# Embedding projection weights moved to a buffer of their own, with first loads, first rounding and last stores reordered

## The reference

```python
def first_block(x, p, ...):
    for i in range(DEPTH):                       # DEPTH = 2
        m = hybrid_mixer(x, ...) if i % 2 == 0 else mla_mixer(x, ...)
        h = layer_norm(DN_ALPHA * x + m, ln1_g[i], ln1_b[i])
        f = jnp.square(jax.nn.relu(h @ mlp_w1[i])) @ mlp_w2[i]
        e = jax.nn.sigmoid(h @ ple_w_gate[i]) * (p[i] @ ple_w_proj[i])   # p[i]: 512 x 256
        x = layer_norm(DN_ALPHA * h + f + e, ln2_g[i], ln2_b[i])
    return x

def second_block(x, c, ctx, ...):
    for layer in range(DEPTH):
        mod_l = (silu(c) @ ada_w[layer] + ada_b[layer]).reshape(batch, 1, 6, D_MODEL)
        ...                                      # mixer with mLSTM, window and full attention
        x = x + mod_l[:, :, 5] * sq_relu_mlp(modulate(x, norm2_g[layer], mod_l, 3), mlp_w1[layer], mlp_w2[layer])
    return x
```

## Time and profile before

| | |
|---|---|
| Runs | 3247.15, 3251.91, 3253.18 us; median 3251.91 us |
| Profiled execution | 3252.88 us, of which the span from the first to the last instruction is 3251.1 us |
| Mean granted TensorE clock | 0.969 of full |
| PE busy | 3072.2 us (94%) |
| DVE, ACT, POOL busy | 1634.8 us (50%), 1233.7 us (38%), 154.0 us (5%) |
| Chain that ended last | PE 86%, DVE 6%, ACT 3%, issue 1%, DMA 1% of the span |

### The profile page before, as it was taken

One profiled execution on the slowest core, in us unless ns is written; L12 is line 12 of the kernel. 1 busy time (PEld: TensorE's weight loads), 2 busy tenths in 40 slices (PEclk: granted clock), 3 DMA queues, 4 the chain that ended last, 5 costly groups with the idle time before them and its releaser, 6 DMA issues.

```text
span 3251.1 us, 39508 instructions
## 1 busy us (share of the span) xinstructions
PE 3072.2 (94%) x15144; PEld 2480.5 (76%) x15144; DVE 1634.8 (50%) x2438; ACT 1233.7 (38%) x2046; POOL 154.0 (5%) x142
## 2 busy tenths in 40 slices
PE   6989999999998999998998998999999899899999
PEld 5676687876776788776885777788888776778887
DVE  4864576775454567775316543433333534344344
ACT  2453233335563233336114442422222344443332
POOL 2300000011000000010002002000000100000000
PEclk9969999999999999999998999999999999999999
DMA  5101434433201344431211001112111110022221
GB/s 193 53 1 58 170 135 180 170 117 52 78 1 58 142 162 181 155 110 40 65 41 38 1 1 52 53 52 77 52 56 73 52 52 27 1 84 97 103 95 59
DMA packets 157680, 259.19 MB, mean 80 GB/s; under 512 B 54333, under 2 KB 70075, under 8 KB 157437
## 3 DMA queue, kind: packets, MB, share of 16 engines
q1 hardware_dynamic: 155812, 252.66, 22.3%
q10 hardware_dynamic: 1628, 4.78, 0.4%
q0 software_dynamic: 128, 0.26, 0.0%
HBM read 255.59 MB, written 2.10 MB: 79 GB/s over the span
## 4 chain that ended last, share of the span: by engine, by line
PE 86%; DVE 6%; ACT 3%; issue 1%; DVEq 1%; DMA 1%; ACTq 1%; POOLq 0%; PEldq 0%; PEld 0%; SPq 0%
PE psA L779 23%; PE psA L780 22%; PE psA L781 22%; PE psB L744 3%; PE psA L730 3%; PE psA L905 3%; PE psO L922 2%; ACT work L1282 2%; PE psO L867 1%; PE psA L966 1%; ACT w_hi L1282 1%; PE psA L795 1%; DVE work L2078 1%; DMA wbuf<-in_hy_w_in_dram 1%; PE psA L797 1%
## 5 line engine op out<-in xcount | busy, mean ns | idle before, releaser
L1282 ACT ACTIVATE w_hi<-wbuf 128x1024 fp32r<-128x1024 f32 (+1 forms) x349 | 368.1, 1057 | 1205.5 <-PE psA L781 1141.6
L779 PE MATMUL psA<-act_hi,w_hi 128*128 128x512 f32 (+1 forms) x1872 | 709.9, 379 | 61.0 <-DVE act_lo L1975 37.6
L1969 DVE TENSOR_TENSOR w_lo<-wbuf,w_hi 128x1024 fp32r<-128x1024 f32 (+1 forms) x349 | 430.3, 1236 | 556.9 <-ACT w_hi L1282 551.9
L780 PE MATMUL psA<-act_lo,w_hi 128*128 128x512 f32 (+1 forms) x1872 | 702.3, 375 | 0.0
L781 PE MATMUL psA<-act_hi,w_lo 128*128 128x512 f32 (+1 forms) x1872 | 700.7, 374 | 0.0
L779 PE MATMUL psA<-hid_hi,w_hi 128*128 128x512 f32 (+1 forms) x1280 | 477.1, 373 | 5.4 <-DVE work L2078 4.5
L780 PE MATMUL psA<-hid_lo,w_hi 128*128 128x512 f32 (+1 forms) x1280 | 472.2, 369 | 0.0
L781 PE MATMUL psA<-hid_hi,w_lo 128*128 128x512 f32 (+1 forms) x1280 | 471.4, 368 | 0.0
L779 PEld LDWEIGHTS psA<-act_hi,w_hi 128*128 128x128 f32 x1872 | 358.9, 192 | 134.3 <-issue 53.3
L780 PEld LDWEIGHTS psA<-act_lo,w_hi 128*128 128x128 f32 x1872 | 358.9, 192 | 62.1 <-issue 1.7
L781 PEld LDWEIGHTS psA<-act_hi,w_lo 128*128 128x128 f32 x1872 | 358.1, 191 | 63.0
(11 more groups left out here) (280 smaller groups left out, 3520.7 us busy)
## 6 DMA issues: line engine op xcount, KB each, us to landing
wbuf<-in_mlp_w_dram SPq DMA_DIRECT2D x64, 2048.0 KB, 8.4
work<-in_ada_w_dram SPq DMA_DIRECT2D x32, 1536.0 KB, 11.2
wbuf<-in_ab_w_in_dram SPq DMA_DIRECT2D x10, 1024.0 KB, 5.1
wbuf<-in_ple_w_gate_dram SPq DMA_DIRECT2D x4, 2048.0 KB, 7.8
wbuf<-in_hy_w_in_dram SPq DMA_DIRECT2D x3, 2048.0 KB, 14.3
wbuf<-in_c_w_in_dram SPq DMA_DIRECT2D x3, 2048.0 KB, 7.8
wbuf<-in_hy_w_out_dram SPq DMA_DIRECT2D x2, 2048.0 KB, 7.8
wbuf<-in_mla_w_out_dram SPq DMA_DIRECT2D x2, 2048.0 KB, 8.1
```

The lines of the kernel that those rows point to most:

```text
L779: pe.matmul(psA[:, s, a:b], w_hi, x_hi[:, a:b], start=first, stop=False)
L780: pe.matmul(psA[:, s, a:b], w_hi, x_lo[:, a:b], start=False, stop=False)
L1282: return nc.scalar.activation(out, in_, func, **kw)
L1969: tt(split_target(wL, stage, u), unit(v, stage, u, g), split_target(wH, stage, u), ALU.subtract).then_inc(S["w_split"], 1)
```

## The change

Three parts. (1) `ple_w_proj` is no longer in the ring: it has 8 KB per partition of working memory of its own (`ple_w`), loaded in one piece ahead of the gate's first chunk once the mixer's output has been split. The products `ple_p` 0 to 3 move into the layer norm: number 0 ahead of the sum of squares, 1 to 3 behind it, into four banks of `psB` and `psO`; DVE multiplies and adds these four between the splits of the gate's weights. Products 4 to 7 stay behind the gate. DVE splits the first two units of the MLP ahead of them, not behind them. (2) At the start a first piece of 256 columns of weights is loaded behind `x` by itself; `ctx`, `p` and the constants are issued only when ACT has split all of `x`; `x` is split tile by tile between the copies, the two first weight units after tiles 2 and 3, and the barrier is gone. (3) The last group of `mlp3` is written out behind the loop, and the transposes of the output stand between its products; ACT copies them to `rows_out` by feature tile, and SP stores four blocks of 256 columns (1 KB per row) in place of four blocks of 128 rows of 4 KB.

The diff, cut to what matters:

```diff
-        chunk("hy", ("split", "hy_xb", 1), (0, *tile_cols(w, 0, 512)))
+        first_w = (wbuf[:, 0, :, 0:256], tile_cols(w, 0, 256)[0])
+        chunk("hy", ("split", "hy_xb", 1), (256, *tile_cols(w, 256, 512)))
...
             for c in range(2):
                 chunk(f"ple{l}", ("split", f"ple_g{l}", 4 * c + 3), (0, *tile_cols(d["ple_w_gate"][l], c * 512, c * 512 + 512)))
-            for c in range(2):
-                chunk(f"ple{l}", (f"ple_p{l}", 4 * c + 3),
-                      (0, *tile_cols(d["ple_w_proj"][l], c * 512, c * 512 + 512, 2)))
...
+        PLE_EARLY = 4
+        ple_banks = [psB[:, 0, :], psB[:, 1, :], psO[:, 512:1024], psO[:, 0:512]]
...
             sp.dma_start(xn, d["x"][0].rearrange("(a p) d -> p a d", p=P)).then_inc(x_in, 16)
+            sp.dma_start(*first_w).then_inc(first_w_in, 16)
...
+                if n in (first_chunk["ple0"], first_chunk["ple1"]):
+                    l = 0 if n == first_chunk["ple0"] else 1
+                    sp.wait_ge(S["act_split"], BASE_X[("hy_out", "mla_out")[l]] + KD)
+                    sp.dma_start(ple_w, d["ple_w_proj"][l].rearrange("(k p) c -> p k c", p=P)).then_inc(ple_w_in, 16)
...
             for t in range(LT):
-                sp.wait_ge(out_set, t + 1)
-                sp.dma_start(out[0][t * P:t * P + P], xn[:, t, :]).then_inc(out_stored, 16)
+                sp.wait_ge(out_set, 2 * t + 2)
+                part = slice(2 * t * P, 2 * t * P + 2 * P)
+                sp.dma_start(out[0].rearrange("(a p) d -> p a d", p=P)[:, :, part], rows_out[:, :, part]).then_inc(out_stored, 16)
...
+            def ple_early(l, js):
+
+                pe.wait_ge(ple_w_in, 16 * (l + 1))
+                for j in js:
+                    if j < 2:
+                        turned(pe, ("dsa_o", "mla_o")[l], (2, 6)[l] + j)
+                    if j == 3:
+                        pe.wait_ge(S["mean_read"], 2 * l + 1)
+                    for k in range(2):
+                        ins = pe.matmul(ple_banks[j], ple_w[:, k, j * P:j * P + P], pT[:, l, k, :],
+                                        start=(k == 0), stop=(k == 1))
+                    ins.then_inc(S["ple_early"], 1)
+
+            def norm_beside_ple(i):
+
+                ple_early(i // 2, [0])
+                layer_norm(i)
+                ple_early(i // 2, range(1, PLE_EARLY))
...
+                def turn_out(j):
+
+                    pe.wait_ge(S["residual_set"], KD + j + 1)
+                    turn("out", j, [(t * P, xT[:, j, t * P:t * P + P]) for t in range(LT)])
...
                         split_products(name, [j0], n, operands, more, [range(GH)])
+                        if leaves:
+                            turn_out(2 * q - 2)
...
+                        if leaves:
+                            turn_out(2 * q - 1)
...
+                leaves = name == "mlp3"
+                with pe.Fori(1 if paired else 0, GROUPS - 1 if leaves else GROUPS) as i:
                     group(i, False)
+                if leaves:
+                    group(GROUPS - 1, False, True)
+                    turn_out(KD - 2)
+                    turn_out(KD - 1)
...
                 split_linear(f"ple_g{l}", sH[LAT], sL[LAT], LAT, split_here(f"mlp{l}"))
-                linear(f"ple_p{l}", f"ple{l}", 2, pT[:, l], LAT, kt=2)
+                for j in range(PLE_EARLY, KD):
+                    product(f"ple_p{l}", j - PLE_EARLY, features(ple_w, j * P, pT[:, l], LAT, 2))
...
             for k in range(KD):
                 turn("load", k, [(t * P, xn[:, t, k * P:k * P + P]) for t in range(LT)])
-            meet(pe)
...
-            layer_norm(0, xT)
+            norm_beside_ple(0)
...
+            def split_first():
+
+                for k in range(KD):
+                    turned(act, "load", k)
+                    f(xH[:, k, :], xT[:, k, 0:LAT], ACT.Copy).then_inc(S["act_hi"], 1)
+                    if k in (2, 3):
+                        w_hi("hy_xa", k - 2)
+
             act.dma_start(const[:, 0:P], consts[:, 0:P]).then_inc(ident_in, 16)
+            split_first()
             act.dma_start(cn, d["ctx_2"][0].rearrange("(a p) d -> p a d", p=P)).then_inc(c_in, 16)
             for l in range(2):
                 act.dma_start(pn[:, l], d["p"][l, 0].rearrange("(a p) d -> p a d", p=P)).then_inc(p_in, 16)
             act.dma_start(const[:, P:], consts[:, P:NCONST]).then_inc(const_in, 16)
-            w_hi("hy_xa", 0)
-            w_hi("hy_xa", 1)
-            meet(act)
...
+            for j in range(KD):
+                ps, free = get_b(act, "out", j)
+                f(rows_out[:, :, j * P:j * P + P], ps.rearrange("p (t c) -> p t c", c=P), ACT.Copy).then_inc(free, 1)
+                act.drain().then_inc(out_set, 1)
...
             def ple(l):
-                split_linear(f"ple_g{l}", start=2)
-                for j in range(KD):
+                def gated_early(j):
+                    if j >= PLE_EARLY:
+                        return
                     emptied(v, f"ple_g{l}", j)
-                    ps, free = get_a(v, f"ple_p{l}", j)
+                    v.wait_ge(S["ple_early"], PLE_EARLY * l + j + 1)
+                    tt(gates[:, j, :], gates[:, j, :], ple_banks[j], ALU.mult)
+                    v.drain()
+                    stt(acc[:, j, :], acc[:, j, :], ALPHA, gates[:, j, :], ALU.mult, ALU.add)
+
+                split_linear(f"ple_g{l}", gated_early, start=2)
+                w_lo(f"mlp{l}", 0)
+                w_lo(f"mlp{l}", 1)
+                for j in range(PLE_EARLY, KD):
+                    emptied(v, f"ple_g{l}", j)
+                    ps, free = get_a(v, f"ple_p{l}", j - PLE_EARLY)
                     tt(gates[:, j, :], gates[:, j, :], ps[:, 0:LAT], ALU.mult).then_inc(free, 1)
                     v.drain()
                     stt(acc[:, j, :], acc[:, j, :], ALPHA, gates[:, j, :], ALU.mult, ALU.add)
                 v.drain().then_inc(S["ple_set"], 1)
-                w_lo(f"mlp{l}", 0)
-                w_lo(f"mlp{l}", 1)
...
             for k in range(KD):
                 ps, free = get_b(v, "load", k)
                 nc.vector.tensor_copy(xT[:, k, 0:LAT], ps).then_inc(free, 1)
-            w_lo("hy_xa", 0)
-            w_lo("hy_xa", 1)
-            meet(v)
+                if k >= 1:
+                    x_lo("hy", k - 1, xT, xH, xL)
+                if k in (2, 3):
+                    w_lo("hy_xa", k - 2)
+            x_lo("hy", KD - 1, xT, xH, xL)
...
             mlp("mlp3", 3, LAT)
-            for t in range(LT):
-                for e in range(2):
-                    ps, free = get_b(v, "out", 2 * t + e)
-                    nc.vector.tensor_copy(xn[:, t, 512 * e:512 * e + 512], ps).then_inc(free, 1)
-                v.drain().then_inc(out_set, 1)
```

42 lines of the change are left out of this document (17 added, 25 removed).

## The result

The changed kernel takes 3222.85 us (median of 4 runs, 3221.17 to 3223.06) against 3249.53 us of the kernel before on the same chip (3247.15 to 3253.18): a ratio of 0.9916, with a 95% interval of 0.9904 to 0.9928. The forecast was 3221. The profiled execution took 3223.06 us, with a span of 3221.2. One run of the last experiment took 4445 us at a mean granted clock of 0.64, in a slow state that says nothing of the code, and is left out of its median.

The account below looks back on a forecast made before the run. PE, busy 94% of the span, bounds the kernel, so only its standing or half-clock time can be won. 19.6 + 4.5 + 3.2 + 1.6 + 2.6 = 31.5 us gives 3221 against 3251.9; own range 3216 to 3227.

Parts of the forecast that it names:

- Handover: Gate to MLP, both layers: PE starts the MLP at T + 8.3 instead of T + 18.1; 9.8 us a layer, 19.6 in all.
- First MLP unit at full clock: First MLP unit, both layers: PE never stands over 1.4 us, so units of 8.03 and 7.35 take 5.45; 4.5 us.
- Norm: First norm, both layers: products fill PE's wait and the clock stays up; 1.6 us a layer, 3.2 in all, from 0.
- Start: Kernel start: `x` lands at 9.2, first product at 23.2 instead of 24.76; 1.6 us won, from -0.6 to 5.
- My sentence that the clock was at its full level before the first transpose: Kernel start: the trace could not test the skill page's rule on transposes, since the clock was already full; no size given.
- rival B: Start gives more: clock up when PE starts the pair saves 2.7 us, sooner `x` up to 5 in all; 3216, chance 0.13.
- End: After the last product: most output transposes move between products, 9.4 us against 12.0; 2.6 us won, between -0.3 and 3.3.
- The 0.4 us for shorter rows: Final store: 0.4 us more, since a 512 KB store now has rows of a quarter the length.
- D: Long stages: denser PE work makes the chip grant less clock; at two points 3282 us; chance 0.03.
- A: Norm and handover: the stall goes but half clock stays, so 4.5 + 3.2 us are not won; 3229, chance 0.14.
- C: Handover: the MLP's first weights still come late because SP is held, so 24.1 us are missing; 3245, chance 0.04.

Follow-up runs that it names:

- the last experiment: Changed kernel, but in layer 1 the MLP's first weights issue only at the gate's end and DVE's low parts follow its pairs: 3226.27 us (median of 3).
- experiment 4: Changed kernel, but all eight projection products stand behind the gate and the MLP's first low parts behind DVE's last pair: 3245.44 us (11 runs).
- experiment 5: Changed kernel, but all eight projection products stand behind the gate, with both MLP low parts ahead of DVE's eight pairs: 3235.26 us (one run).
- the end alone: Kernel before with only the new end (transposes between last products, copies on ACT, stores by columns): 3245.02 us (11 runs), ratio 0.9988.
- the start alone: Kernel before with only the new start (loads, splitting, barriers): 3245.6 us (median of 11 runs), ratio 0.9997.
- both orders: Changed kernel with the MLP's second low part behind the four pairs and the first weights' splits placed later at the start: 3215.11 us (4 runs).
- experiment 8: Changed kernel with two extra matmuls in layer 1 (3223.27 us), with four (3231.97), unchanged again (3222.13), and with layer 1's MLP weights issued late (3226.27).
- the second trace of the changed kernel: Changed kernel run once more, nothing altered: median 3222.13 us; the profiled execution took 3227.75 us.

## Why the prediction was right

**Handover: right, 19.6 us.** The MLP starts at T + 8.3 as worked out, T being the gate's end, and the one wait left is that of product 6 for DVE. What the working did not say is how the 9.8 us part: by experiments 4 and 5 the transfer taken away alone gives little, and the four products moved into the norm, once it is gone, give most.

**First MLP unit at full clock: 4.5 forecast.** True in the changed kernel (5.5 us in both layers), but the code of before loses less there than its one trace said: in layer 0 the first unit took 8.03 us in that trace and 7.15 in the trace of the end alone. Against the trace of the end alone both handovers with their first units give 11.2 + 11.5 = 22.7 us, beside 24.1 for the two terms together.

**Norm: the term that failed.** The step said that the clock stays up and each norm gains 1.6. The clock stays up. But the second trace with the old norm is itself 1.3 us faster there, because its clock is back before the last tile is split; then both kernels wait for that tile, and in layer 0 nothing is gained. In layer 1 it is 0.8 us (lead from 18.7 to 19.5). So the two norms gave some 0.8 in place of 3.2; the lower bound was 0, but for another reason than the one given ("the clock still falls").

**Start: 3.5 by the medians, 4.0 between traces, 1.6 forecast.** `x` at 9.12 for 9.2 and the splits as ordered; the two waits for ACT and the copies made 13.3 us of chain to the first product in place of 14.0, and the pair took 11.0 us where 12.1 was kept. The clock at the start has to be read with care. In the trace of the start alone the column says 1.00 throughout, and the chain says otherwise:

```profile
20.00:21.00 1.00, 0.92 (x5) 0.52 (x5) 1.00 (x3) 0.43 (x2) 0.00 (x0) 1.00 1.26 176
```

```profile
8.87 1.95 PE psB L750 x8
...
20.93 1.12 PE psB L750 x4
22.05 0.43 PE psA L785
...
24.93 0.23 PE psA L786
```

A product takes 0.43 us until 24.6 and 0.23 after it, and a transpose 0.24 to 0.28 us (1.95 / 8, 1.12 / 4) where one at the end takes 0.11 (0.44 / 4): here PE is at half clock from its first transpose to behind its first product, and the column shows 1.00 only because no change has been recorded yet. My sentence that the clock was at its full level before the first transpose rested on that column, and was wrong. But it is not the same in each trace. The transposes of the kernel before (first row) and of the changed kernel (the other two):

```profile
17.91 0.66 PE L744 MATMUL psB<-const,work 128*128 128x128 f32 x4 [0.19 <-DVE xT L2153]
```

```profile
13.18 0.66 PE L756 MATMUL psB<-const,work 128*128 128x128 f32 x4 [0.25 <-DVE xT L2204]
16.64 1.11 PE L756 MATMUL psB<-const,work 128*128 128x128 f32 x4 [2.81 <-DVE xT L2204]
```

Four transposes in 0.66 us are at full clock (0.11 from one to the next), four in 1.11 at half (0.21). In the kernel before the clock is low for the first 24 transposes, rises at 17.1 and falls at 20.5, while PE stands. In the changed kernel it rises at 12.6, behind some fifteen transposes, falls at 16.0 in a wait, and rises again at 26.3. PE had done nothing but transposes when it rose. The Trainium skill, page "TensorE: Matmul & The Clock Gate", section "Part 4: PE-mode transpose", has it that transposes are no work for the clock. The trace of the start alone looks like that (32 transposes left it low); ten of the fourteen traces, these two among them, do not, and they decide. So it was not that rule that kept the first half of rival B, a clock that is up when the pair starts, from coming: the clock was up and fell again in the waits between the transposes. With the first product it was up in one trace only, that of both orders (up from 13.4, down at 20.2, 0.5 us behind the first product). It rose 2.6 us behind the first product in the trace of the start alone, 3.8 in the changed kernel, and 5.9 before. The difference of the last two, 2.1 us at half clock, is 1.0 of the 1.1 us by which the pair was faster than I had kept it, and was in no term of the forecast.

**End: 3.3 between traces, 4.1 by the medians, 2.6 forecast.** From DVE's last addition on 6.3 us (6.4 forecast); the six turns cost 0.44 each in place of 0.5. The 0.4 us for shorter rows stood on no row; from the end of ACT's last copy (3217.82) to the end of the span it is 3.4 us, where 3.1 and 0.4 were reckoned.

**The sum.** 31.5 us were forecast; 26.7 were measured on the chip of the result, and 26.3 against the median of 27 runs of before. The total came out because two errors met, and that part is luck: the terms together were 5.2 us too high, and the starting point, 3252.9, was 3.8 above the median of those 27 runs, 3249.1. The 5.2 are made up of 1.4 too much for the handovers with their first units, 2.4 too much for the norms (for the most part clock losses that the one profiled execution of before had and another did not), and some 2.8 at two small stages that no term had; against them stand 1.9 too little for the start and 0.7 to 1.5 too little for the end. That leaves 1 to 2 us that no run puts in a place. D, less clock in the long stages, did not come; the small loss of its kind came in the short ones. A and C did not come; of B, 1.9 us more than forecast at the start.

## What to carry to other kernels

A transfer in the chain is not its own length in price: take it away and the chain goes through what stood beside it, so ask first what is late then. The price also depends on the order in which the parts are taken: here the transfer alone gave 0.7 to 2.7 us, and in layer 1 a late transfer put back beside the four early products cost 5.8. Work that is put into a wait that exists anyway, and is in nobody's way there (four products in the norm), is worth its full time where it stood before, 6.9 us; and between two engines, the short operation that frees a slot goes first, and one that is wanted a unit later goes last. Before a term is taken from one trace, look at the same place in a second execution, since what a stall costs in clock differs between them (3 us of standing cost 5.8 in one run here, 1.2 us cost nothing more).

## What the runs showed of the hardware

The loss to a low clock at the first two small stages of experiment 8 was 1.7, 3.4 or 5.1 us of full clock in all fourteen traces, with nothing between; at later stages the same program differs by the same amounts from one execution to the next. Over the whole span 99.9 us of full clock are missing in the second trace of the changed kernel and 90.5 in the first, and 4.7 us of that showed in the time.

The clock also falls while PE is busy without a gap. In the changed kernel:

```profile
1582.89 2.38 PE L1201 MATMUL psB<-const,work 4*128 4x4 f32 x36
```

```profile
1580.00:1586.00 6.00, 6.00 (x69) 5.87 (x67) 1.85 (x2) 1.06 (x1) 0.00 (x0) 1.00 0.00 0
```

PE is busy for 6.00 of these 6.00 us and for 10.00 of 10.00 in the window from 1584 to 1594; it does 4x4 products from 1582.89 and 4x12 products behind them, the clock falls near 1586, and the next 128x512 matmuls run at half clock. No idle time stands ahead of this fall.

The clock can rise while PE does nothing but 128x128 transposes (at 12.6 us in the changed kernel, at 17.1 in the kernel before), and the same start left it low through all 32 of them in other executions (the start alone).

A 1 MB transfer queued behind 2 MB on the same queue took 16.1 us to land with 4.5 MB on another queue beside it, and at most 12.4 without them (issued at 1.25, split at 13.69): the second queue delayed these bytes by at least 3.6 us, and `x`, ahead of them, by 2.3 (first transpose at 11.51 for 9.25).

The clock column reads 1.00 until the first change is recorded, whatever the clock is; the duration of a matmul of known shape tells it (0.43 us for 128x512 at a column of 1.00 in the trace of the start alone, 0.23 from 24.9 on).
